# Attention steps of four jobs instead of two, in both halves of the PSUM banks

## The reference, cut to what matters

```
layer 0: s = q @ k * scale - slope * dist, masked to a window of 128
         m = max(max(s), sink); p = exp(s - m); p = p / (sum(p) + exp(sink - m)); out = p @ v
layer 1: p = softmax(...) for c = 0, 1; a = p[0] - lam * p[1]; o = a @ v; rms_norm over each head of 128
memory:  p = softmax(q_mem @ km * scale); out = p @ vm
both:    x = LN(ALPHA * x + concat(out) @ w_out); x = LN(ALPHA * x + moe(x))
```

## Time and profile before

| | |
|---|---|
| median of 3 runs | 1216.44 us (1216.11 to 1217.76) |
| the profiled execution | 1215.17 us, its span 1213.2 us |
| TensorE busy | 1165.9 us, 96% of the span |
| VectorE, ScalarE, GpSimd busy | 349.1, 303.8, 64.4 us |
| granted TensorE clock | 0.997 of full |
| attention steps of layer 0 | about 33 to 109 us of the span |
| attention steps of layer 1 | about 625 to 706 us |
| expert stages | about 145 to 592 us and 755 to 1201 us |

### The profile page before, as it was taken

How to read it: one execution, slowest core, us unless ns; L and a number is a source line. 1 busy time by engine, 2 the same in 40 slices (tenths; PEclk the granted TensorE clock), 3 DMA queues, 4 the chain that set the end, 5 groups by cost and what they waited for, 6 DMA issues and landing times.

```text
span 1213.2 us, 22689 instructions
## 1 busy us (share of the span) xinstructions
PE 1165.9 (96%) x8946; PEld 707.8 (58%) x8948; DVE 349.1 (29%) x904; ACT 303.8 (25%) x713; POOL 64.4 (5%) x102
## 2 busy tenths in 40 slices
PE   9999999999999999998999999999999899999985
PEld 6764855555555555554687748555555555555552
DVE  1334622222122212221523456121222222222214
ACT  1444212222121212221223432121221222122212
POOL 1331000000001000000012100000000010000000
PEclk9999999999999999999999999999999999999998
DMA  9942799999999999999990468999999999999995
GB/s 359 363 173 105 292 412 419 422 421 422 423 421 420 411 422 420 422 422 420 389 363 22 151 252 346 400 419 420 422 421 422 422 419 407 397 421 422 421 420 207
DMA packets 74503, 446.92 MB, mean 368 GB/s; under 512 B 6977, under 2 KB 12481, under 8 KB 24897
## 3 DMA queue, kind: packets, MB, share of 16 engines
q1 hardware_dynamic: 72208, 441.22, 89.0%
q10 hardware_dynamic: 2224, 4.72, 1.0%
HBM read 444.86 MB, written 1.05 MB: 368 GB/s over the span
## 4 chain that ended last, share of the span: by engine, by line
PE 71%; DMA 18%; issue 6%; DVE 3%; POOL 2%; SPq 0%; ACT 0%; DVEq 0%; POOLq 0%
DMA ring<-in_w_up 17%; PE bank L1237 16%; PE bank L1218 14%; PE bank L1271 14%; PE bank L748 6%; PE bank L1279 4%; PE bank L767 4%; PE bank L806 4%; PE bank L1244 1%; POOL soft L707 1%; PE bank L1094 1%; PE bank L782 1%; PE bank L1117 1%; DMA ring<-in_w_in_a 1%; PE bank L1304 1%
## 5 line engine op out<-in xcount | busy, mean ns | idle before, releaser
L1237 PE MATMUL bank<-ring,work 128*64 128x256 f32 x1952 | 225.3, 379 | 13.8 <-DMA ring<-in_w_up 13.8
L1218 PE MATMUL bank<-ring,work 128*64 128x256 f32 x1984 | 227.8, 382 | 8.7 <-DMA ring<-in_w_gate 8.5
L1271 PE MATMUL bank<-ring,work 128*32 128x512 f32 x1904 | 222.0, 595 | 0.2
L1218 PEld LDWEIGHTS bank<-ring,work 128*64 128x64 f32 x1984 | 141.3, 137 | 116.6 <-issue 57.8
L1237 PEld LDWEIGHTS bank<-ring,work 128*64 128x64 f32 x1952 | 147.1, 137 | 81.9 <-issue 20.3
L1934 DVE SCALAR_TENSOR_TENSOR yhalf<-bank,gcol,yhalf 128x512 fp32r<-128x512 f32 x124 | 93.0, 750 | 214.4 <-ACT yhalf L1560 214.4
L1926 DVE TENSOR_TENSOR work<-work,bank 128x256 f32<-128x256 f32 x64 | 27.0, 421 | 366.8 <-PE bank L1237 366.8
L1560 ACT ACTIVATE yhalf<-bank,gcol 128x512 fp32r<-128x512 f32 x124 | 85.4, 689 | 181.2 <-PE bank L1271 181.2
L1271 PEld LDWEIGHTS bank<-ring,work 128*32 128x32 f32 x1904 | 57.4, 109 | 116.9 <-issue 110.0
L1401 ACT ACTIVATE work<-bank 128x512 f32<-128x512 f32 (+4 forms) x177 | 78.0, 441 | 101.5 <-PE bank L748 44.6
L1401 ACT ACTIVATE back<-bank 128x128 fp32r<-128x128 bf16 x64 | 17.8, 278 | 280.3 <-PE bank L1190 280.3
(11 more groups left out here) (190 smaller groups left out, 849.6 us busy)
## 6 DMA issues: line engine op xcount, KB each, us to landing
ring<-in_w_gate SPq DMA_DIRECT2D x124, 1024.0 KB, 13.7
ring<-in_w_up SPq DMA_DIRECT2D x122, 1024.0 KB, 15.5
ring<-in_w_down SPq DMA_DIRECT2D x119, 1024.0 KB, 14.5
ring<-in_w_in_b SPq DMA_DIRECT2D x3, 3072.0 KB, 18.6
ring<-in_w_out SPq DMA_DIRECT2D x4, 2048.0 KB, 13.1
home<-in_w_gate SPq DMA_DIRECT2D x4, 1024.0 KB, 17.4
ring<-in_w_down SPq DMA_DIRECT2D x8, 512.0 KB, 13.3
ring<-in_w_in_a ACTq DMA_DIRECT2D x1, 3072.0 KB, 19.6
```

The source lines that it names most:

```text
L1218: last = pe.matmul(gate_bank[slots_of(e), 0:HID], xg[:, k, slots_of(2 * j + e)], w[e][:, k, :], start=(k == 0), stop=(k == KT - 1))
L1237: last = pe.matmul(up_bank[slots_of(e), 0:HID], xg[:, k, slots_of(2 * j + e)], w[e][:, k, :], start=(k == 0), stop=(k == KT - 1))
L1271: last = pe.matmul(yb[half][rows_of(t, e), :], hT[b][:, f, slots_of(e, t)], w[e][:, f, half * 512:half * 512 + 512], start=(f == 0), stop= ...
```

## The change

A step takes four jobs, the two pairs that stood in two steps before (`BATCH = 4`). There are 8 batches and 10 steps of a layer. Nothing is computed differently, and each matmul, copy and exponential is issued as before.

- The second pair of a batch uses the other half of each bank: columns 256 on for scores and transposes, 128 on for the value products. Two more buffers of transposed probabilities are added, over memory that `memnat` held.
- TensorE: all transposes of batch d - 2, a filler, all value products of batch d - 2, all scores of batch d. VectorE: four additions, four maxima, four `soften`. ScalarE: four copies of transposes, four exponentials, four head copies.
- Waits go by batch: VectorE's additions wait for all four scores, ScalarE's copies for the last transpose (or last product) of the batch, and the next scores for all four reads.
- The fillers are cut anew: each step of a batch has about what two steps had. The four transposes of memory rows move from three steps into step 1 of layer 0, ahead of the third query projection, into banks 2, 3, 6 and 7.
- The heads that layer 1 normalises first are 10 instead of 11, and 2 instead of 1 come late. TensorE's wait for 19 heads stays.

```diff
-HEADS_EARLY, HEADS_LATE = slice(0, 11), slice(11, 12)
+HEADS_EARLY, HEADS_LATE = slice(0, 10), slice(10, 12)
+BATCH = 4
+        def half_of(s):
+            return s % BATCH // 2
+
+        def score_at(s, w):
+            return banks[4 + s % 2][:, half_of(s) * 256:half_of(s) * 256 + w]
+
+        def first_product(l, j):
+            return len([q for q in products[l] if batch_of(q) < batch_of(j)])
+
+        def last_product(l, j):
+            return len([q for q in products[l] if batch_of(q) <= batch_of(j)])
...
-                job_pairs = [(j, j + 1) for j in range(0, J, 2)]
-                for i in range(len(job_pairs) + 2):
-                    filler_ahead(i)
-                    if i >= 2:
-                        for j in job_pairs[i - 2]:
-                            turn(j)
-                    filler(i)
-                    if i >= 2:
-                        values(job_pairs[i - 2])
-                    if i < len(job_pairs):
-                        scores(job_pairs[i])
+                batches = [[(j, j + 1) for j in range(b, b + BATCH, 2)] for b in range(0, J, BATCH)]
+                for d in range(len(batches) + 2):
+                    filler_ahead(d)
+                    if d >= 2:
+                        for pair in batches[d - 2]:
+                            for j in pair:
+                                turn(j)
+                    filler(d)
+                    if d >= 2:
+                        for pair in batches[d - 2]:
+                            values(pair)
+                    if d < len(batches):
+                        for pair in batches[d]:
+                            scores(pair)
...
+                def filler_0(d):
+                    if d == 0:
+                        tiles("q1", wq, 256, xT, 0, 16)
+                    elif d == 1:
                         pe.wait_ge(sem("mem_in"), 16)
+                        for n in range(4):
                             turn_rows(memnat, G[0, "mem"] + n, n // 2, n % 2)
+                        tiles("q2", wq, 512, xT, 0, 6)
+                    elif d == 2:
+                        tiles("q2", wq, 512, xT, 6, 16)
...
+                    elif d == 8:
                         out_part(1, (3, 4))
                         headed(4 * 5 + 2)
                         out_part(0, (5,))
                         out_part(1, (5,))
+                    elif d == 9:
                         pe.wait_ge(sem("score_read"), base + J)
                         headed(4 * 5 + 4)
+                        out_part(2, (0, 1, 2, 3, 4, 5))
                         out_part(3, (0,))
...
+                    elif d == 7:
                         headed(8)
                         out_part(0, (6,))
                         out_part(1, (6,))
+                    elif d == 8:
+                        out_part(0, (7,))
                         out_part(1, (7,))
+                    elif d == 9:
                         out_part(3, (6,))
...
-                    act.wait_ge(sem("turning"), m + 1)
-                    if m >= 2:
-                        act.wait_ge(sem("valued"), m - 1)
+                    act.wait_ge(sem("turning"), pbase + last_product(l, j))
+                    if batch_of(j) > 0 or l > 0:
+                        act.wait_ge(sem("valued"), pbase + first_product(l, j))
...
-                    act.wait_ge(sem("valued"), m + 1)
+                    act.wait_ge(sem("valued"), pbase + last_product(l, j))
...
-                    dve.wait_ge(sem("scored"), s + 1)
+                    dve.wait_ge(sem("scored"), base + BATCH * (batch_of(j) + 1))
...
+                for d in range(J // BATCH + 1):
+                    if d >= 1:
+                        a, b, c, e = range(BATCH * (d - 1), BATCH * d)
+                        for j in (a, b, c, e):
                             bias(j)
+                        for j in (a, b, c, e):
                             maximum(j)
+                        for j in (a, b, c, e):
                             soften(j)
+                    fillers_out(d)
```

More of the change, by code:

```diff
@@ L113, in build_trunk @@
     ]
+    HEADS_BASE = len(products[1]) - TT * DIFF_HEADS
     G, readers, bank_no = {}, "", []
@@ L193, in build_trunk @@
         soft = [over(f"soft{i}", [P, 256], xhalf_at + 1024 * i) for i in range(3)] + [work[:, 8450:8706]]
-        softT = [over(f"softT{i}", [P, 2, P], xhalf_at + 4096 + 1024 * i) for i in range(2)]
+        softT = [over(f"softT{i}", [P, 2, P], xhalf_at + at) for i, at in enumerate((4096, 5120, 14336, 15360))]
         negmax = sb("negmax", [P, 32])
@@ L877, in filler_0 @@
                         part_landed(pe, (0, "in1"), 1)
[L878 to L881, removed]
+                        tiles("qm", wm, 0, xT, 0, 14)
+                    elif d == 4:
+                        tiles("qm", wm, 0, xT, 14, 16)
                         landed(pe, (0, "memkv"))
[L883 to L900, removed]
+                        memory_keys(0, 11)
+                    elif d == 5:
+                        memory_keys(11, 16)
+                        memory_values(0, 9)
+                    elif d == 6:
+                        memory_values(9, 16)
+                        headed(4 * 1 + 2)
+                        out_part(0, (0, 1))
+                    elif d == 7:
@@ L957, in filler_1, with filler_ahead @@
                         out_part(3, (6,))
[L959 to L963, removed]
+                def filler_ahead(d):
+                    if l == 0 and d == 2:
+                        for n in range(4):
+                            evacuated(pe, G[0, "mem"] + n)
+                    elif l == 1 and d == 9:
                         pe.wait_ge(sem("score_read"), base + J)
@@ L987, in scores @@
                     if base + pair[0] > 0:
-                        pe.wait_ge(sem("score_read"), base + pair[0])
+                        pe.wait_ge(sem("score_read"), base + batch_of(pair[0]) * BATCH)
                     for j in pair:
@@ L1026, in values @@
                             kind, h, n, c = jobs[l][j]
[L1027 removed]
+                            dst, probs = value_at(l, j), softT[(m0 + i) % BATCH][:, t, :]
                             if kind == "mem" or l == 0:
@@ L1492, in head_out @@
                     else:
-                        copy(heads[:, n, h * P:(h + 1) * P], bank[:, 0:P])
+                        copy(heads[:, n, h * P:(h + 1) * P], src)
                         act.wait_ge(sem("headed"), m)
-                        last = act.activation(square, bank[:, 0:P], ACT.Square, accum_out=hsq[:, TT * h + n:TT * h + n + 1])
+                        last = act.activation(square, src, ACT.Square, accum_out=hsq[:, TT * h + n:TT * h + n + 1])
                     last.then_inc(sem("headed"), 1)
-                for i in range(J // 2 + 2):
-                    if i >= 2:
-                        for j in (2 * i - 4, 2 * i - 3):
+                last_d = J // BATCH
@@ L1501, in _ @@
+                for d in range(last_d + 2):
+                    ready = range(BATCH * (d - 2), BATCH * (d - 1))
+                    if d >= 2:
+                        for j in ready:
                             turned(j)
-                    if 1 <= i < J // 2 + 1:
-                        for j in (2 * i - 2, 2 * i - 1):
+                    if 1 <= d <= last_d:
+                        for j in range(BATCH * (d - 1), BATCH * d):
                             exps(j)
-                    fillers_out(i)
@@ L1506, in _ @@
-                    if i >= 2:
-                        for j in (2 * i - 4, 2 * i - 3):
+                    fillers_out(d)
+                    if d >= 2:
+                        for j in ready:
                             head_out(j)
-                    if l == 1 and i >= J // 2:
-                        part = (HEADS_EARLY, HEADS_LATE)[i - J // 2]
-                        act.wait_ge(sem("headed"), pbase + len(products[l]) - 1 + (i - J // 2))
+                    if l == 1 and d >= last_d:
+                        part = (HEADS_EARLY, HEADS_LATE)[d - last_d]
+                        act.wait_ge(sem("headed"), pbase + part.stop + HEADS_BASE)
@@ L1763, in soften @@
                            .then_inc(sem("softened"), 1)
-                for i in range(J // 2 + 1):
-                    if i >= 1:
-                        for j in (2 * i - 2, 2 * i - 1):
+                for d in range(J // BATCH + 1):
+                    if d >= 1:
+                        a, b, c, e = range(BATCH * (d - 1), BATCH * d)
+                        for j in (a, b, c, e):
                             bias(j)
-                        for j in (2 * i - 2, 2 * i - 1):
+                        for j in (a, b, c, e):
                             maximum(j)
-                        for j in (2 * i - 2, 2 * i - 1):
+                        for j in (a, b, c, e):
                             soften(j)
-                    fillers_out(i)
+                    fillers_out(d)
                 if l == 1:
```

(2 more changed lines are left out.)

147 lines of the change are left out of this document (62 added, 85 removed), and 2 rows, old and new, of the table plan.

## The result

| | before | after |
|---|---|---|
| median | 1216.12 us (5 runs, 1215.62 to 1217.76) | 1209.24 us (5 runs, 1208.90 to 1209.74) |
| the profiled execution | 1215.17 us, span 1213.2 | 1209.24 us, span 1207.3 |
| ratio | | 0.9944, 95% interval 0.9931 to 0.9957 |

The kernel is 6.9 us faster by medians and 5.9 us by the two traces. I had predicted 2.95 us less, 1213.5 us, and 1211.5 as the lowest. The direction was right, the gain is more than twice the forecast, and the time lies outside my range. Of all runs of this document one, of the kernel before beside e1 to e4, took 4137.19 us where its neighbours took 1215 to 1219; it is left out of every median.

What follows compares the result with a forecast made beforehand. TensorE's hand-written order was taken to bound the attention steps, each microsecond counting one for one. Layer 0's -2.45 and layer 1's -0.5 us sum to -2.95, a median of 1213.5 us, range 1211.5 to 1218.

Steps and rivals of the forecast that it cites:

- layer 0, groups joined: Layer 0's 8 batches: three groups of small matmuls instead of six save 0.51 us each, -4.1 us.
- step 1: Layer 0: last job's softmax ready at 6.05 us, its transposes due at 5.8, so TensorE waits +0.35 us.
- step 8: Layer 0, a step without scores: last transposes due at 6.3 us, ready at 7.1, +0.8 us.
- layer 1, groups joined: Layer 1: joined groups save 2.1 us in 6 self batches and 1.0 in 2 memory batches, -3.1 us.
- step 8, last transpose of batch 6: Layer 1: batch 6 ready for its last transpose at 5.8 us, due at 3.8 to 3.9, +1.95 us.
- step 8 and 9, batch 7: Layer 1: VectorE free for batch 7 only at 5.8 us; ready at 11.5, TensorE there at 10.4, +1.1 us.
- How long a batch's softmax takes: Summed durations after the scores: layer 0 self batch ready at 6.05 us, memory at 7.0, layer 1 self at 5.8.
- The seven new waits: TensorE's new stalls in both layers: 0.35, 0.8, 0.8, 1.95, 1.1, 0.2 and 0.85, together 6.05 us.
- The first: Rival: once-paid time stays with each pair, so only stalls change: +4.25, 1220.7 us; chance 6%.
- The second: Rival: batch softmax longer than summed, both layers' ends pay; at 1.1 us more, +2.5, 1219 us; chance 12%.
- third: Rival: batch softmax longer than summed by only 0.3 us: -1.5, 1215 us; chance 18%.
- fourth: Rival: the expert stream, waiting for DMA anyway, takes the gain back: 0, 1216.4 us; chance 14%.

Runs made afterwards that it cites:

- e1: Changed kernel, but TensorE alternates values and scores pair by pair inside a step, softmax still by batches of four; median 1214.63 us.
- e4: Changed kernel with the short steps at the ends of both layers filled by projection work moved there; median 1209.22 us.
- e2: Changed kernel with 16 more matmuls that nobody reads ahead of layer 0's second step; median 1213.66 us.
- e5: Changed kernel with layer 1's fifth query projection moved from step 6 to 7 and output projection work ahead of the wait for the nineteenth head; median 1208.99 us.
- e8: The kernel before, unaltered, run and traced once more; median 1215.72 us.

## Why the prediction was right in kind and too small

By its own terms, with what the two traces show from the start of one group to the start of the next:

| term | predicted | measured |
|---|---|---|
| layer 0, groups joined | -4.1 | -3.9 |
| old waits of layer 0 | -0.3 | -0.7 |
| step 1 | +0.35 | +0.07 |
| step 8 | +0.8 | +0.43 |
| head copies behind step 9 | +0.8 | +0.69 |
| **layer 0** | **-2.45** | **-3.5** |
| layer 1, groups joined | -3.1 | -2.9 |
| old waits of layer 1 | -1.5 | -1.5 |
| step 8, last transpose of batch 6 | +1.95 | +1.32 |
| step 8 and 9, batch 7 | +1.1 | +0.43 |
| square root and its table | +0.2 | 0 |
| wait for 19 heads | +0.85 | +0.62 |
| VectorE's heads ahead of `turn_heads` | not seen | -0.6 |
| **layer 1** | **-0.5** | **-2.6** |

The measured terms sum to -3.4 in layer 0 and -2.6 in layer 1, against totals of -3.5 and -2.6.

**The groups were right** (7.2 predicted, 6.8 measured), and with them the choice between the two rules of the Trainium skill. The Trainium skill, page TensorEngine Tiling (Array Packing), section Tiling Modes, has a change of mode drain the engine. The runs agree with it so far as they go: e1 puts those changes back and pays 3.81 us for them; a drain as such shows in no row. The Trainium skill's rule on weight loads pulled ahead of matmuls (page TensorE: Matmul & The Clock Gate, section Part 2: What happens when you issue a matmul) does not hide this.

**The step that failed is "How long a batch's softmax takes".** The seven new waits were forecast at 6.05 us in all and came to 3.56. The last softmaxes of layer 1 after the change show why (timeline of VectorE, then of GpSimd; TensorE's scores ended at 688.10):

```profile
688.25 1.15 DVE L1739 SCALAR_TENSOR_TENSOR acc<-negdist,bank 128x128 f32<-128x128 f32 x4 [3.41 <-PE bank L993]
689.31 1.12 DVE L1750 TENSOR_REDUCE negmax<-acc 128x1 f32<-128x128 f32 x4
690.36 0.34 DVE L1757 RECIPROCAL rden<-rowsum 128x1 f32<-128x1 f32 x2
...
692.93 0.48 DVE L1764 SCALAR_TENSOR_TENSOR work<-work,rden,soft 128x256 f32<-128x256 f32 x1 [0.88 <-POOL soft L731]
693.33 1.14 DVE L1739 SCALAR_TENSOR_TENSOR acc<-negdist,bank 128x128 f32<-128x128 f32 x4
```

```profile
690.60 0.60 POOL L731 TENSOR_SCALAR soft<-acc,rden 128x128 f32<-128x128 f32 x1 [6.72 <-DVE rden L1757]
691.87 0.92 POOL L731 TENSOR_SCALAR soft<-acc,rden 128x256 f32<-128x256 f32 x1 [0.66 <-DVE rden L1757]
```

```profile
693.47 0.44 PE L1004 MATMUL bank<-ident,work 128*128 128x128 f32 x2 [1.32 <-DVE work L1764]
```

I had added the durations of instructions that overlap. Two additions of 256 last 0.75 us, but the maxima behind them begin 0.67 after their start: what a pair costs its queue is 0.67, not 0.75. Four additions and four maxima were taken as 2.45 us and take 690.36 - 688.25 = 2.11 (each row of the timeline begins before the last one's end). GpSimd starts at 2.5 after the scores, not 2.8; its second multiplication at 3.8, not 4.2; the last combination ends at 5.3, not 5.8. TensorE was there at 4.05 and not at 3.85, so 1.95 became 1.32: 0.4 of it by the softmax, 0.2 by TensorE. Batch 7 begins on VectorE that much earlier and is shorter itself: 1.1 became 0.43. In step 8 of layer 0 GpSimd was done 6.7 us behind the scores, not 7.1: 0.8 became 0.43. It is the lever that I had named myself ("each microsecond of latency above my sums costs some 5 us"), and it worked downwards: 0.2 to 0.5 us of latency less in each softmax stands behind most of the 1.95 us by which these waits and step 1's are under the forecast, out of 2.5 us for all seven.

**Step 1 of layer 0** shows it most simply. GpSimd's last multiplication ended 5.86 us behind the scores, not 6.05, and the last transposes began at 5.92, where I had them due at 5.8: the wait of 0.35 went to 0.07.

**What I had not seen at all are waits that the list of TensorE's waits leaves out**, since it goes by the matmuls. In layer 0 a second wait of before stood behind the listed one: from the two transposes at 52.76 us to the next record it is 0.59 us instead of 0.27, because GpSimd's second result comes late. In layer 1 TensorE's weight loads waited for the heads that VectorE normalises, and for a copy by VectorE behind them. The weight loads of before:

```profile
53.19 0.14 PEld L1009 LDWEIGHTS bank<-ident,soft 128*128 128x128 f32 x1 [0.29 <-POOL soft L707]
...
706.26 0.85 PEld L1067 LDWEIGHTS bank<-ident,heads 128*128 128x128 f32 x4
...
708.62 0.30 PEld L806 LDWEIGHTS bank<-ring,work 128*128 128x128 f32 x2 [0.26 <-DVE work L1641]
```

And the first four head transposes' weight loads after:

```profile
701.14 0.42 PEld L1065 LDWEIGHTS bank<-ident,heads 128*128 128x128 f32 x4 [0.81 <-ACT work L1495]
```

The same four loads take 0.85 us before and 0.42 after. An idle time ahead of a weight load is not by itself such a wait: ahead of the last head transposes of before, at 711.73 and 712.16 us, 0.24 and 0.29 us stand with "issue" beside them, and no matmul is late. What counts is how far apart the matmuls start. From the first head transposes to the long stretch of output projection behind the last, it took 712.59 - 706.37 = 6.22 us before and 706.81 - 701.14 = 5.67 after, some 0.6 less: about 0.26 in the first four transposes, 0.2 ahead of the projection at 708.62. After the change TensorE comes to these transposes later against VectorE, 1.8 us behind its first normalised head (699.37 us) and not 0.6 (705.78), since it has just waited for the heads' copies. The head that moved from the early to the late ones has no part in this: VectorE had it behind the copy.

**The rivals.** The first (time paid per pair) is refuted by the group sizes and e1. The second (a longer softmax) has the right place and the wrong sign. The third and fourth forecast less gain than mine; e2 refutes the fourth. None of my cases lay on the side on which the error was: I had made the low end of the range only from stalls that stay away by a third, and they stayed away by 2.5 of 6.05 us, with another 1 us of old waits and heads on top.

## What to carry to other kernels

Where small groups of matmuls of another tile form stand between long ones, count the groups, not the instructions: each costs 0.15 to 0.21 us here (0.05 to 0.09 where the form is the filler's), and joining two of a kind gives that back as long as a filler covers the longer hand-over. Work a chain of hand-overs out from starts to starts, never from sums of durations, and give the low end of the range the same multiplier as the high end. Before a stage that is bound by TensorE is taken at its waits as listed, compare the starts of a group with those of its like elsewhere: a wait can stand at the weight loads alone. And look in the kernel at what an instruction waits for before a releaser's name is believed.

## What the runs showed of the hardware

- TensorE's granted clock fell to half, its lower level of 1.2 GHz, after a wait of 2.22 us (e5) and of 2.46 us (e8) for an up weight late in layer 0's expert stage; after one of 2.27 us, 20 us earlier in the stage (the first trace of before), and after those of 1.77 us or less it did not. The 32 products behind it took 5.36 us instead of 3.67. A stream that is just in time can so turn 0.8 us of lateness into 2.5 us.
- A program's own stages repeat within 0.2 us from trace to trace where TensorE bounds them, and within 2.3 us where it waits for loads. To compare two kernels by one trace each, compare the stages and leave out those that the change does not touch.
